# Matmuls on 64 rows of the PE array: from alternating between its two halves into two PSUM banks, to one half after the other into one bank

## Chip, cores, metric

One core of a Trainium2 chip runs the whole program once. The metric is the device time of that run in microseconds (us), median of three runs.

## What is computed

Two transformer-like blocks of two layers each, on 512 tokens of width 1024, in float32. Only the mixer of the first block matters here. It has three branches: sliding-window attention, HGRN2 and a gated delta rule (GDN). The parts around the change are these:

```python
# HGRN2: per head, dk = 64
attn = einsum('bhtd,bhsd,bhtsd->bhts', q, k, decay)   # decay = exp(cum_t - cum_s), causal
# gated delta rule: per head, dk = 64
A  = where(strict, einsum('bnhtd,bnhsd->bnhts', k * beta, k) * L, 0)
qk = where(incl,   einsum('bnhtd,bnhsd->bnhts', q, k) * L, 0)
```

Each branch has four heads of dimension 64, and the kernel works on chunks of 128 tokens (the reference uses 64). So every product in question is 128x128 with a contraction over 64.

## The kernel before

The five engines run programs written by hand, joined by semaphores. `at[key]` is a mark (semaphore, count), `wait_ge` waits for it, and `own()` lets an engine wait for the completion of its own last instruction. Each phase has a `main` stream (gemms with weights from a ring of three DMA buffers) and side streams (`conv`, `gdn`, `att`, `hgrn`, `inv`, `mem`). `weave` interleaves their generator steps into one order, the same on all engines, from hand-given costs. The change leaves each step's counts of instructions and its declared costs as they are, and so this order too.

Head h sits in partitions 64*(h%2) to 64*(h%2)+63. Its matmul therefore uses only the upper or only the lower 64 rows of the PE array. One float32 matmul is two MATMUL records in the trace, each with its own weight load. PSUM has 8 banks of 128x512 float32. `take` hands out a stream's banks in turn and lets PE wait until the one it hands out has been read: `hgrn` has two (6 and 7), `gdn` two (2 and 3).

Three groups of matmuls are touched, in both layers of the first block:

- `diag` (`hgrn_pe`): k times q for 4 chunks x 4 heads, 16 matmuls a layer; DVE multiplies them by the identity into `ACC` (4 instructions of 512 columns).
- `lev` (`hgrn_pe`): 14 steps a layer (7 levels x 2 pairs of heads) of 8 matmuls; DVE copies their masked parts over `ACC` with two `copy_predicated` (line 168).
- `kk` (`gdn_pe`): 4 steps a layer of 8 matmuls; DVE turns them into `AT` (k k) and `G5` (q k), 8 instructions of 512 columns.

In all three, PE takes both banks of the pool first. It then alternates: a matmul on the upper rows into the first bank, one on the lower rows into the second. DVE reads each bank with a pattern that puts the heads in place. For the other matmuls of this shape, in `ob`, `vn` and `og`, the kernel already has the order that the change brings: heads `HO = (0, 2, 1, 3)` with `own()` before head 1. All matmuls and transposes of the side streams go through `mm` and `tr` (lines 103 and 109); gemms are line 570.

Of the kernel before, what the change touches and what calls it, by code (L numbers as in the profile page):

```python
# [8 lines left out]
I32 = mybir.dt.int32  # L9
ALU = mybir.AluOpType  # L10
# [27 lines left out]
HO = (0, 2, 1, 3)  # L38
# [177 lines left out]
def bc(ap, axis, n):  # L216
    v = ap.unsqueeze(axis)
    shape = list(v.shape)
    shape[axis] = n
    return v.to_broadcast(shape)  # L220
# [65 lines left out]
def program(nc, T, out):  # L286
    ctx = ExitStack()
    with ctx:
# [48 lines left out]
        at = Marks()  # L337
        bank_of, plans = {}, {}
# [6 lines left out]
        ident = cst[:, K_ID:K_ID + 128]  # L345
# [6 lines left out]
        LV = [cst[:, K_LV + 128 * i:K_LV + 128 * (i + 1)] for i in range(7)]  # L352
# [468 lines left out]
        ACC = ar(O_HG + 7168, 4, 512)  # L821
# [354 lines left out]
        def hgrn_dve(v, l):  # L1176
# [34 lines left out]
                sl = slice(128 * i, 128 * i + 128)  # L1211
                at["cum", l] = v.scan(CUM[:, sl], ones, Zb[:, sl], par=True)
            yield
            A5 = ACC.rearrange("p c (i h t) -> p c i h t", i=2, h=2)
            id4 = ident.unsqueeze(1).unsqueeze(1).to_broadcast([128, 2, 2, 128])
            for c in range(0, 4, 2):
                for p in range(2):
                    v.wait_ge(at["diag", l, c, p])
                    at["free", ("diag", l, c, p)] = v.tt(
                        A5[:, c:c + 2, :, p], bank_of["diag", l, c, p].rearrange("p (c i t) -> p c i t", c=2, i=2), id4, ALU.mult,  # L1220
                        par=True)
            yield

            def halves(n):
# [7 lines left out]
            for s in range(-2, 15):  # L1232
                if 0 <= s < 14:
                    _, (_, (ef, es), (xf, xs), (_, qs), (kf, _)) = halves(s)
                    v.wait_ge(at["levexp", l, s], at["lev", l, s - 2] if s > 1 else None)
                    v.tt(xs, qs, es, ALU.mult, par=True)
                    at["levx", l, s] = v.tt(xf, kf, ef, ALU.mult, par=True)
                if s + 2 < 14:
                    hb, ((cf, cs), (ef, es), _, _, _) = halves(s + 2)
                    ref = cf[:, :, hb - 1:hb].to_broadcast([128, 256 // hb, hb])  # L1240
                    if s >= 0:
                        v.wait_ge(at["levx", l, s])
                    v.tt(es, cs, ref, ALU.subtract, par=s > -2)
                    at["leve", l, s + 2] = v.tt(ef, ref, cf, ALU.subtract, par=True)
                if s == 13:
                    at["lev_dve", l] = v.now()
                if 1 <= s < 15:
                    lv, i = LEV[s - 1]
                    mk = bc(LV[lv].bitcast(I32), 1, 4)
                    for h in range(2):  # L1250
                        v.wait_ge(at["lev", l, s - 1, h])
                        at["lev_acc", l] = at["free", ("lev", l, s - 1, h)] = v.pred(
                            A5[:, :, i, h], mk, bank_of["lev", l, s - 1, h].rearrange("p (c t) -> p c t", c=4))
                yield
            v.wait_ge(at["ecum", l])
            v.tt(BQ, BQ, E_, ALU.mult, par=True)
# [27 lines left out]
        def hgrn_pe(pe, l):  # L1284
            yield (5 if l == 0 else 9, 5 if l == 0 else 7)
            yield (3.5, 0)
            for c in range(0, 4, 2):
                pair = [take(pe, ("diag", l, c, p), "hgrn") for p in range(2)]
                pe.wait_ge(at["cum", l], at["hz", l])
                for u in range(4):  # L1290
                    ti, cs = u % 2, slice((c + u // 2) * 128, (c + u // 2) * 128 + 128)
                    for p in range(2):
                        rows = slice(64 * p, 64 * p + 64)
                        at["diag", l, c, p] = pe.mm(pair[p][:, u * 128:(u + 1) * 128], [(KT3[rows, ti, cs], BQ3[rows, ti, cs])])
            yield (2.8, 0)
            for s in range(-2, 15):
                if 1 <= s < 15:
                    lv, i = LEV[s - 1]
                    X3 = XV[:, 512 * i:512 * i + 512]
                    pair = [take(pe, ("lev", l, s - 1, h), "hgrn") for h in range(2)]  # L1300
                    pe.wait_ge(at["levx", l, s - 1])
                    for c in range(4):
                        for h in range(2):
                            x = X3[64 * h:64 * h + 64, c * 128:(c + 1) * 128]
                            at["lev", l, s - 1] = at["lev", l, s - 1, h] = pe.mm(pair[h][:, c * 128:(c + 1) * 128], [(x, x)])
                yield (3.2, 0.7)
            yield (3.8, 3)
            yield (1.3, 1.1)
            for m in range(0, 4, 2):
                bank = take(pe, ("kd", l, m), "hgrn")  # L1310
                pe.wait_ge(at["kdec", l])
                for u in range(4):
                    at["kd_t", l, m] = pe.tr(bank[:, u * 128:(u + 1) * 128],
                                             KT3[:, u % 2, (m + u // 2) * 128:(m + u // 2) * 128 + 128], ident)
            yield (1.5, 0)
            for c in range(6):
                if c < 4:
                    b, b2 = take(pe, ("ob", l, c), "hgrn"), take(pe, ("os", l, c), "hgrn")
                    pe.wait_ge(at["kd", l], at["hv", l])
                    for h in range(4):  # L1320
                        pr, ti = (h % 2) * 64, h // 2
                        hs = slice(64 * h, 64 * h + 64)
                        at["os", l, c] = pe.mm(b2[pr:pr + 64, ti * 64:ti * 64 + 64], [(KD[:, c, hs], BV3[:, c, hs])])
                    pe.wait_ge(at["st", l, c], at["lev_acc", l])
                    for h in HO:
                        pr, ti = (h % 2) * 64, h // 2
                        hs = slice(64 * h, 64 * h + 64)
                        if h == 1:
                            pe.own()
                        at["ob", l, c] = pe.mm(b[:, hs], [  # L1330
                            (ACC[:, c, h * 128:(h + 1) * 128], BV3[:, c, hs]),
                            (BQ3[pr:pr + 64, ti, c * 128:(c + 1) * 128], STs[c % 2][pr:pr + 64, ti, :])])
                if c in (3, 5):
                    finish_pe(pe, l, "h", c - 3, OB)
                yield (2.2, 1.5)
# [65 lines left out]
        def gdn_pe(pe, l):  # L1401
# [31 lines left out]
                        at["tr_t", l, m, half] = pe.tr(bank[:, u * 128:(u + 1) * 128],  # L1433
                                                       src[:, (u % 2) * 128:(u % 2) * 128 + 128], ident)
            yield (0, 1.1)
            for n in range(4):
                m0, which = n // 2 * 2, n % 2
                pair = [take(pe, ("kk", l, n, p), "gdn") for p in range(2)]
                pe.wait_ge(at["tr", l, m0 + 1])
                for u in range(4):  # L1440
                    m, ti = m0 + u // 2, u % 2
                    for p in range(2):
                        rows = slice(64 * p, 64 * p + 64)
                        at["kk", l] = at["kk", l, n, p] = pe.mm(pair[p][:, u * 128:(u + 1) * 128], [
                            (TR[rows, m, 2 + ti, :], TR[rows, m, (4 if which == 0 else 0) + ti, :])])
                yield (2.4, 0)
            for m in range(4):
                yield (1.5, 0)
# [82 lines left out]
        def gdn_act(a, l):  # L1531
# [41 lines left out]
                yield  # L1573
            for m in range(5):
                if m:
                    a.wait_ge(at["tm_t", l, m - 1], at["kk", l])
                    at["tm", l, m - 1] = at["free", ("tm", l, m - 1)] = a.cp(TM[:, m - 1, :], bank_of["tm", l, m - 1][:, :], par=True)
                yield

# [47 lines left out]
        def gdn_dve(v, l):  # L1627
# [41 lines left out]
            for m in range(4):  # L1669
                v.wait_ge(at["tr_t", l, m, 0])  # L1670
                k = hd(TOK[:, m, 256:512])
                v.tt(k, k, bc(eD[:, 4 * m:4 * m + 4], 2, 64), ALU.mult, par=True)
                m0, which = m // 2 * 2, m % 2
                v.wait_ge(at["g5e", l, m0 + 1])
                if which:
                    v.own()
                for p in range(2):
                    a4, g4 = [z[:, m0:m0 + 2, :].rearrange("p m (i h t) -> p m i h t", i=2, h=2)[:, :, :, p] for z in (AT, G5)]
                    k4 = bank_of["kk", l, m, p].rearrange("p (m i t) -> p m i t", m=2, i=2)
                    v.wait_ge(at["kk", l, m, p])  # L1680
                    if which == 0:
                        t = v.stt(a4, k4, -1.0, g4, ALU.mult, ALU.mult, par=True)
                    else:
                        t = v.tt(g4, k4, g4, ALU.mult, par=True)
                    at["free", ("kk", l, m, p)] = t
                yield
            v.own()
            v.wait_ge(at["kk", l])
            for m in range(5):
                if m < 4:  # L1690
                    a4, t4 = [z[:, m, :].rearrange("p (h t) -> p h t", h=4) for z in (AT, TT)]
# [1314 lines left out]
```

## Time and profile before

| | |
|---|---|
| median of three runs | 4441.57 us (4433.45, 4441.57, 4442.74) |
| the profiled run's own time | 4433.45 us |
| its span in the profile | 4431.7 us |
| granted TensorE clock, mean over the span | 0.945 of 2.4 GHz |

The span is the time from the first to the last instruction in the profile; 1.75 us of the run lie outside it. Idle times in brackets in the views name what ended them.

### The profile page before, as it was taken

Reading aid. Unit: us, or ns where it says so; the run is one execution under the profiler, and the core shown is the slowest. Engines: PE = TensorE matmul, PEld = TensorE weight load, DVE = VectorE, ACT = ScalarE, POOL = GpSimd, SP = SyncE. Lnnn points to the kernel's source line nnn. Section 1 sums busy time; section 2 is a strip of 40 time slices with the busy share of each in tenths; the row PEclk is TensorE's granted clock in tenths of the full one; section 3 lists DMA queues with packets and bytes.
Section 4 is the critical chain, followed back from the end, with each engine's and each line's share of the span. In section 5 each row is a group of like instructions: output and inputs, shape, how many; then the busy total and the mean of one; then the engine's idle time right before and its main releaser. Section 6 shows DMA issues by size and latency. Waiting matters only on the chain.

```text
span 4431.7 us, 51774 instructions
## 1 busy us (share of the span) xinstructions
PE 4051.1 (91%) x20660; PEld 3326.6 (75%) x20660; DVE 2573.7 (58%) x4060; ACT 1639.0 (37%) x2880; POOL 107.7 (2%) x199
## 2 busy tenths in 40 slices
PE   5878979988879899999999999999899999999998
PEld 4757868867659778888888777767778787777776
DVE  6775455554675332346666744676566667445865
ACT  2343232233443232333434233453344343334532
POOL 0000000000000000000000000000000000000000
PEclk9978889999979799989999999999899999999999
DMA  6402135633202133323231233133242312231233
GB/s 219 148 15 67 44 119 189 191 124 96 72 10 77 58 95 96 98 93 105 81 105 58 81 91 91 53 108 119 70 132 78 109 60 84 81 91 62 78 105 121
DMA packets 216641, 417.93 MB, mean 94 GB/s; under 512 B 16384, under 2 KB 61472, under 8 KB 214608
## 3 DMA queue, kind: packets, MB, share of 16 engines
q1 hardware_dynamic: 197584, 335.12, 24.4%
q0 software_dynamic: 18816, 79.49, 5.2%
q8 instruction: 163, 2.67, 0.2%
q14 instruction: 78, 0.64, 0.0%
HBM read 378.89 MB, written 35.67 MB: 94 GB/s over the span
## 4 chain that ended last, share of the span: by engine, by line
PE 75%; DVE 15%; ACT 6%; DMA 2%; issue 2%; DVEq 0%; SPq 0%; ACTq 0%; POOLq 0%
PE ps L570 55%; PE ps L103 14%; DVE arena L120 4%; ACT arena L191 3%; PE ps L109 3%; DVE arena L135 3%; DVE spl L120 3%; PE ps L2142 2%; ACT sph L191 1%; DMA ring<-in_ada_w 1%; DVE sm L141 1%; DVE HF L120 1%; DVE X L120 1%; PE ps L2138 1%; DVE arena L129 0%
## 5 line engine op out<-in xcount | busy, mean ns | idle before, releaser
L120 DVE TENSOR_TENSOR spl<-ring,sph 128x1024 fp32r<-128x1024 f32 (+2 forms) x556 | 651.6, 1179 | 834.7 <-ACT sph L191 833.3
L191 ACT ACTIVATE sph<-ring 128x1024 fp32r<-128x1024 f32 (+2 forms) x556 | 562.2, 1021 | 878.6 <-PE ps L570 668.2
L570 PE MATMUL ps<-sph,HTh 128*128 128x512 f32 (+3 forms) x1728 | 685.5, 397 | 10.7 <-ACT sm L191 5.4
L570 PE MATMUL ps<-spl,HTh 128*128 128x512 f32 (+3 forms) x1728 | 638.6, 370 | 0.0
L570 PE MATMUL ps<-sph,HTl 128*128 128x512 f32 (+3 forms) x1728 | 637.5, 369 | 0.0
L191 ACT ACTIVATE arena<-ps 128x512 f32<-128x512 f32 (+2 forms) x574 | 316.9, 564 | 778.6 <-PE ps L570 479.2
L570 PE MATMUL ps<-HTh,sph 128*128 128x512 f32 x1376 | 548.4, 399 | 23.1 <-DVE spl L120 16.0
L570 PE MATMUL ps<-HTh,spl 128*128 128x512 f32 x1376 | 540.1, 393 | 0.0
L570 PE MATMUL ps<-HTl,sph 128*128 128x512 f32 x1376 | 540.0, 392 | 0.0
L103 PE MATMUL ps<-arena 64*128 64x128 f32 (+7 forms) x2328 | 410.5, 368 | 55.7 <-ACT arena L191 22.3
L570 PE MATMUL ps<-sph 128*128 128x512 f32 x992 | 402.4, 406 | 8.8 <-DVE spl L120 8.7
L570 PEld LDWEIGHTS ps<-sph,HTh 128*128 128x128 f32 x1728 | 339.2, 196 | 83.7 <-issue 32.9
L570 PE MATMUL ps<-sph,spl 128*128 128x512 f32 x992 | 391.8, 395 | 0.0
L103 PEld LDWEIGHTS ps<-arena 64*128 64x128 f32 (+2 forms) x2328 | 296.2, 211 | 127.2 <-issue 28.9
L570 PE MATMUL ps<-spl,sph 128*128 128x512 f32 x992 | 390.5, 394 | 0.0
L570 PEld LDWEIGHTS ps<-sph,HTl 128*128 128x128 f32 x1728 | 339.5, 196 | 62.9 <-issue 18.8
L570 PEld LDWEIGHTS ps<-spl,HTh 128*128 128x128 f32 x1728 | 338.4, 196 | 53.3
L570 PEld LDWEIGHTS ps<-HTh,sph 128*128 128x128 f32 x1376 | 261.4, 190 | 78.6 <-DVE spl L120 22.7
L570 PEld LDWEIGHTS ps<-HTh,spl 128*128 128x128 f32 x1376 | 260.9, 190 | 55.7
L570 PEld LDWEIGHTS ps<-HTl,sph 128*128 128x128 f32 x1376 | 261.3, 190 | 53.1 <-issue 1.0
L109 PE MATMUL ps<-cst,arena 128*128 128x128 f32 x1160 | 186.7, 298 | 117.9 <-ACT arena L191 73.2
L109 PEld LDWEIGHTS ps<-cst,arena 128*128 128x128 f32 x1160 | 146.4, 153 | 168.0 <-ACT arena L191 71.0
(195 smaller groups left out, 5293.6 us busy)
## 6 DMA issues: line engine op xcount, KB each, us to landing
ring<-in_w_in SPq DMA_DIRECT2D x264, 512.0 KB, 3.7
ring<-in_ada_w SPq DMA_DIRECT2D x96, 512.0 KB, 4.4
ring<-in_w_down SPq DMA_DIRECT2D x44, 512.0 KB, 3.3
ring<-in_w_gate SPq DMA_DIRECT2D x40, 512.0 KB, 4.2
ring<-in_w_up SPq DMA_DIRECT2D x40, 512.0 KB, 4.6
ring<-in_w_mem SPq DMA_DIRECT2D x32, 512.0 KB, 3.4
ring<-in_w_out SPq DMA_DIRECT2D x32, 512.0 KB, 3.7
ring<-in_w_br_ssd SPq DMA_DIRECT2D x32, 512.0 KB, 3.8
```

Source lines behind the costliest of these rows:

```text
L103: ins = self.e.matmul(o, l, r, start=i == 0, stop=stop)
L109: self.e.transpose(o, i, ident).then_inc(*self.done.up())
L120: self.e.tensor_tensor(o, a, b, op).then_inc(*self.done.up())
L135: self.e.scalar_tensor_tensor(out=o, in0=a, scalar=s1, in1=b, op0=op0, op1=op1).then_inc(*self.done.up())
L141: self.e.tensor_reduce(o, a, AX, op).then_inc(*self.done.up())
L191: self.e.activation(o, a, f, **kw).then_inc(*self.done.up())
L570: ins = pe.e.matmul(o, l, r, start=k0 == 0 and i == 0 and not b.pairs, stop=k0 + b.ks == b.kt and i == 3 * b.ks - 1 and (c0 > 0 or not b.p ...
L2138: pe.e.matmul(bank.rearrange("p (h t) -> p h t", h=4), NFr[0][:, :], bc(NFr[1 + d][:, :], 1, 4), start=True, stop=False)
L2142: ins = pe.e.matmul(bank[:, h * 128:(h + 1) * 128], AA[:, m, h0 + h:h0 + h + 1].to_broadcast([128, 128]), tri, start=False, stop=h == 3)
```

## The change

It gives up the alternation. `diag` now fills one bank per chunk with the four heads in the order 0, 2 (upper rows), `own()`, 1, 3 (lower rows). `lev` fills one bank per two chunks: two matmuls on the upper rows, `own()`, two on the lower ones. `kk` fills one bank per chunk m and kind (k k or q k), in the order of `diag`, and its step m waits for the transposes of chunk m alone. Banks are taken one at a time. The numbers of matmuls (16, 112, 32 a layer) and of DVE instructions stay; their patterns change, and DVE waits for its own previous instruction before each `G5` product (four a layer, before two and one after them).

```diff
-            for c in range(0, 4, 2):
-                pair = [take(pe, ("diag", l, c, p), "hgrn") for p in range(2)]
+            for c in range(4):
+                bank = take(pe, ("diag", l, c), "hgrn")
                 pe.wait_ge(at["cum", l], at["hz", l])
-                for u in range(4):
-                    ti, cs = u % 2, slice((c + u // 2) * 128, (c + u // 2) * 128 + 128)
-                    for p in range(2):
-                        rows = slice(64 * p, 64 * p + 64)
-                        at["diag", l, c, p] = pe.mm(pair[p][:, u * 128:(u + 1) * 128], [(KT3[rows, ti, cs], BQ3[rows, ti, cs])])
+                for h in HO:
+                    pr, ti = (h % 2) * 64, h // 2
+                    if h == 1:
+                        pe.own()
+                    at["diag", l, c] = pe.mm(bank[:, h * 128:(h + 1) * 128], [
+                        (KT3[pr:pr + 64, ti, c * 128:(c + 1) * 128], BQ3[pr:pr + 64, ti, c * 128:(c + 1) * 128])])
...
-                    pair = [take(pe, ("lev", l, s - 1, h), "hgrn") for h in range(2)]
-                    pe.wait_ge(at["levx", l, s - 1])
-                    for c in range(4):
+                    for c in range(0, 4, 2):
+                        bank = take(pe, ("lev", l, s - 1, c), "hgrn")
+                        pe.wait_ge(at["levx", l, s - 1])
                         for h in range(2):
-                            x = X3[64 * h:64 * h + 64, c * 128:(c + 1) * 128]
-                            at["lev", l, s - 1] = at["lev", l, s - 1, h] = pe.mm(pair[h][:, c * 128:(c + 1) * 128], [(x, x)])
+                            for u in range(2):
+                                x = X3[64 * h:64 * h + 64, (c + u) * 128:(c + u + 1) * 128]
+                                if h and not u:
+                                    pe.own()
+                                at["lev", l, s - 1] = at["lev", l, s - 1, c] = pe.mm(
+                                    bank[:, (2 * u + h) * 128:(2 * u + h + 1) * 128], [(x, x)])
...
-            for n in range(4):
-                m0, which = n // 2 * 2, n % 2
-                pair = [take(pe, ("kk", l, n, p), "gdn") for p in range(2)]
-                pe.wait_ge(at["tr", l, m0 + 1])
-                for u in range(4):
-                    m, ti = m0 + u // 2, u % 2
-                    for p in range(2):
-                        rows = slice(64 * p, 64 * p + 64)
-                        at["kk", l] = at["kk", l, n, p] = pe.mm(pair[p][:, u * 128:(u + 1) * 128], [
-                            (TR[rows, m, 2 + ti, :], TR[rows, m, (4 if which == 0 else 0) + ti, :])])
+            for m in range(4):
+                for which in range(2):
+                    bank = take(pe, ("kk", l, m, which), "gdn")
+                    pe.wait_ge(at["tr", l, m])
+                    for h in HO:
+                        pr, ti = (h % 2) * 64, h // 2
+                        if h == 1:
+                            pe.own()
+                        at["kk", l, m, which] = pe.mm(bank[:, h * 128:(h + 1) * 128], [
+                            (TR[pr:pr + 64, m, 2 + ti, :], TR[pr:pr + 64, m, (4 if which == 0 else 0) + ti, :])])
                 yield (2.4, 0)
...
-                    for h in range(2):
-                        v.wait_ge(at["lev", l, s - 1, h])
-                        at["lev_acc", l] = at["free", ("lev", l, s - 1, h)] = v.pred(
-                            A5[:, :, i, h], mk, bank_of["lev", l, s - 1, h].rearrange("p (c t) -> p c t", c=4))
+                    for c in range(0, 4, 2):
+                        v.wait_ge(at["lev", l, s - 1, c])
+                        at["lev_acc", l] = at["free", ("lev", l, s - 1, c)] = v.pred(
+                            A4[:, c:c + 2], mk, bank_of["lev", l, s - 1, c].rearrange("p (c h t) -> p c h t", c=2, h=2))
```

## Rows read from the trace of the kernel before

**Rows 1.** The page: its head and its chain by engine.
```profile
span 4431.7 us, 51774 instructions
...
PE 75%; DVE 15%; ACT 6%; DMA 2%; issue 2%; DVEq 0%; SPq 0%; ACTq 0%; POOLq 0%
```
**Rows 2.** Windows: busy (records) of PE, PEld, DVE, ACT, POOL; clock; DMA share, GB/s.
```profile
264.00:280.00 16.00, 12.49 (x58) 9.22 (x58) 10.97 (x24) 6.30 (x17) 0.00 (x0) 0.53 0.01 2
...
364.00:400.00 36.00, 32.59 (x186) 28.16 (x186) 16.52 (x30) 14.01 (x25) 0.56 (x1) 0.71 0.18 59
```
**Rows 3.** Waits of PE from 240 to 365 us: total us, times, longest.
```profile
PE ps L109 <- ACT arena L191: 12.3, 4, 4.9
...
PE ps L103 <- DVE sm L120: 4.7, 1, 4.7
...
PE ps L103 <- DVE arena L168: 2.5, 1, 2.5
PE ps L103 <- DVE sm L135: 1.9, 1, 1.9
```
**Rows 4.** The chain that ended last, 262 to 284 us: start, us, what.
```profile
264.08 5.51 PE ps L103 x24
...
281.97 1.14 PE ps L103 x16
283.11 1.32 DVE arena L168 x2
```
**Rows 5.** The same chain, a piece near 296 us, then 339 to 365 us.
```profile
295.80 1.09 PE ps L103 x16
...
340.96 2.01 PE ps L103 x16
...
345.07 5.01 PE ps L103 x52
...
356.99 1.21 DVE HF L135 x2
...
358.33 5.68 PE ps L103 x20
```
**Rows 6.** Timeline, two `kk` steps on PE: start, us, engine, line, form, records.
```profile
348.91 1.16 PE L103 MATMUL ps<-X 64*128 64x128 f32 x16
...
358.33 2.08 PE L103 MATMUL ps<-X 64*128 64x128 f32 x16 [5.56 <-DVE HF L135]
```
**Rows 7.** Timeline, PE on products of all 128 rows, one after another.
```profile
269.51 1.97 PE L109 MATMUL ps<-cst,arena 128*128 128x128 f32 x8
...
277.95 1.12 PE L109 MATMUL ps<-cst,arena 128*128 128x128 f32 x4
...
409.53 0.39 PE L103 MATMUL ps<-X,arena 128*128 128x128 f32 x2
409.75 0.39 PE L103 MATMUL ps<-arena,X 128*128 128x128 f32 x2
```
**Rows 8.** Timeline, PE before and after `own()` in an `ob` step.
```profile
375.26 0.69 PE L103 MATMUL ps<-sm,arena 64*128 64x64 f32 x2
376.00 0.69 PE L103 MATMUL ps<-arena 128*128 128x64 f32 x2
```
**Rows 9.** Timeline, a `lev` step on PE and its two DVE reads.
```profile
312.96 3.35 PE L103 MATMUL ps<-arena 64*128 64x128 f32 x19
...
315.15 1.33 DVE L168 COPY_PREDICATED arena<-cst,ps 128x512 f32<-128x512 int32 x2
```
**Rows 10.** PE groups by form in 331.2 to 331.75 us: busy, mean ns.
```profile
L103 PE MATMUL ps<-arena 64*128 64x256 f32 x4 | 1.0, 376 | 0.0
L103 PE MATMUL ps<-arena 64*128 64x128 f32 x5 | 0.7, 286 | 0.0
```
**Rows 11.** The chain at `diag` of the second layer.
```profile
1153.76 1.28 DVE arena L120 x2
...
1155.17 2.02 PE ps L103 x24
```

More of the change, by code:

```diff
@@ L1213, in hgrn_dve @@
             yield
-            A5 = ACC.rearrange("p c (i h t) -> p c i h t", i=2, h=2)
-            id4 = ident.unsqueeze(1).unsqueeze(1).to_broadcast([128, 2, 2, 128])
-            for c in range(0, 4, 2):
-                for p in range(2):
[L1218 to L1221, printed above, removed]
+            for c in range(4):
+                v.wait_ge(at["diag", l, c])
+                at["free", ("diag", l, c)] = v.tt(
+                    ACC[:, c, :].rearrange("p (h t) -> p h t", h=4), bank_of["diag", l, c].rearrange("p (h t) -> p h t", h=4),
+                    bc(ident, 1, 4), ALU.mult, par=True)
             yield
@@ L1248, in hgrn_dve @@
                     lv, i = LEV[s - 1]
-                    mk = bc(LV[lv].bitcast(I32), 1, 4)
-                    for h in range(2):
-                        v.wait_ge(at["lev", l, s - 1, h])
-                        at["lev_acc", l] = at["free", ("lev", l, s - 1, h)] = v.pred(
-                            A5[:, :, i, h], mk, bank_of["lev", l, s - 1, h].rearrange("p (c t) -> p c t", c=4))
+                    A4 = ACC.rearrange("p c (i h t) -> p c i h t", i=2, h=2)[:, :, i]
+                    mk = LV[lv].bitcast(I32).unsqueeze(1).unsqueeze(1).to_broadcast([128, 2, 2, 128])
+                    for c in range(0, 4, 2):
+                        v.wait_ge(at["lev", l, s - 1, c])
+                        at["lev_acc", l] = at["free", ("lev", l, s - 1, c)] = v.pred(
+                            A4[:, c:c + 2], mk, bank_of["lev", l, s - 1, c].rearrange("p (c h t) -> p c h t", c=2, h=2))
                 yield
@@ L1286, in hgrn_pe @@
             yield (3.5, 0)
-            for c in range(0, 4, 2):
-                pair = [take(pe, ("diag", l, c, p), "hgrn") for p in range(2)]
+            for c in range(4):
+                bank = take(pe, ("diag", l, c), "hgrn")
                 pe.wait_ge(at["cum", l], at["hz", l])
-                for u in range(4):
-                    ti, cs = u % 2, slice((c + u // 2) * 128, (c + u // 2) * 128 + 128)
-                    for p in range(2):
-                        rows = slice(64 * p, 64 * p + 64)
-                        at["diag", l, c, p] = pe.mm(pair[p][:, u * 128:(u + 1) * 128], [(KT3[rows, ti, cs], BQ3[rows, ti, cs])])
+                for h in HO:
[4 more added lines that the diff above has]
+                        (KT3[pr:pr + 64, ti, c * 128:(c + 1) * 128], BQ3[pr:pr + 64, ti, c * 128:(c + 1) * 128])])
             yield (2.8, 0)
@@ L1435, in gdn_pe @@
             yield (0, 1.1)
-            for n in range(4):
-                m0, which = n // 2 * 2, n % 2
-                pair = [take(pe, ("kk", l, n, p), "gdn") for p in range(2)]
-                pe.wait_ge(at["tr", l, m0 + 1])
-                for u in range(4):
-                    m, ti = m0 + u // 2, u % 2
-                    for p in range(2):
-                        rows = slice(64 * p, 64 * p + 64)
-                        at["kk", l] = at["kk", l, n, p] = pe.mm(pair[p][:, u * 128:(u + 1) * 128], [
-                            (TR[rows, m, 2 + ti, :], TR[rows, m, (4 if which == 0 else 0) + ti, :])])
+            for m in range(4):
[8 more added lines that the diff above has]
+                            (TR[pr:pr + 64, m, 2 + ti, :], TR[pr:pr + 64, m, (4 if which == 0 else 0) + ti, :])])
                 yield (2.4, 0)
@@ L1575, in gdn_act @@
                 if m:
-                    a.wait_ge(at["tm_t", l, m - 1], at["kk", l])
+                    a.wait_ge(at["tm_t", l, m - 1], at["kk", l, 3, 1])
                     at["tm", l, m - 1] = at["free", ("tm", l, m - 1)] = a.cp(TM[:, m - 1, :], bank_of["tm", l, m - 1][:, :], par=True)
@@ L1672, in gdn_dve @@
                 v.tt(k, k, bc(eD[:, 4 * m:4 * m + 4], 2, 64), ALU.mult, par=True)
[L1673 to L1680, printed above, removed]
+                v.wait_ge(at["g5e", l, m])
+                for which in range(2):
+                    v.wait_ge(at["kk", l, m, which])
                     if which == 0:
-                        t = v.stt(a4, k4, -1.0, g4, ALU.mult, ALU.mult, par=True)
+                        t = v.stt(AT[:, m, :], bank_of["kk", l, m, 0][:, :], -1.0, G5[:, m, :], ALU.mult, ALU.mult, par=True)
                     else:
-                        t = v.tt(g4, k4, g4, ALU.mult, par=True)
-                    at["free", ("kk", l, m, p)] = t
+                        t = v.tt(G5[:, m, :], bank_of["kk", l, m, 1][:, :], G5[:, m, :], ALU.mult)
+                    at["free", ("kk", l, m, which)] = t
                 yield
-            v.own()
-            v.wait_ge(at["kk", l])
+            v.wait_ge(at["kk", l, 3, 1])
             for m in range(5):
```

## The prediction

> **What bounds the kernel now.** I read the page first. PE makes up 75% of the chain that ended last, DVE 15% [rows 1]. The average says little here, because all three groups sit in the mixers of the first block. So I went through the mixers by windows, waits and chain.
>
> From about 240 to 365 us (and again in the second layer, where every reading below repeats unless I say otherwise; I looked it up and don't show it) no engine is full. The chain jumps between PE, DVE and ACT, and PE runs much of the time at the lower of its two clock levels: 264 to 280 us shows a granted clock of 0.53, nearly all of it at 1.2 GHz [rows 2]. PE also waits a lot there, four times for ACT (12.3 us) and singly for DVE for 4.7, 2.5 and 1.9 us [rows 3]. The reader should see two kinds of touched steps. In some the chain runs through their matmuls; in others PE idles soon after, so that a longer step is hidden.
>
> **What one touched step costs now.** A `lev` or `kk` step is 8 matmuls, 16 records. It spans 1.16 us at the full clock and 2.08 us at the lower one [rows 6]. Products on all 128 rows, which nothing can run beside, start one per 0.22 us, two records of 0.11 [rows 7]. Eight would take 1.8 us, so the 1.16 us show that upper and lower rows now work side by side: eight turns of 0.11 plus about 0.27 to fill and drain. At the lower clock four more transposes take 1.97 - 1.12 = 0.85 us, a turn of 0.21 [rows 7].
>
> **What one costs after.** Two matmuls on the same rows are a block of four turns. At full clock that is 1.16 less four turns, 0.71; a block has half as many record starts to offset, so I take 0.68. At the lower clock it is 2.08 - 0.85 = 1.23. Behind `own()` the next matmul starts about 0.05 us after the last one ends: 375.26 + 0.69 = 375.95, next at 376.00 [rows 8]. A step is then: upper block of bank one, `own()`, lower block of bank one beside the upper block of bank two (other rows, other bank, no wait between them), `own()`, lower block of bank two. That is three blocks and two handovers. Full clock: 3 x 0.68 + 0.1 = 2.15, 1.0 us more than now. Lower clock: 3 x 1.23 + 0.1 = 3.8, 1.7 us more.
>
> That the middle blocks really overlap I take from 331.2 to 331.75 us, where four records of 64x256 on one half and five of 64x128 on the other ran in the same 0.55 us [rows 10].
>
> The Trainium skill (TensorE: Matmul & The Clock Gate, Part 3, The mechanism) says that matmuls start and end strictly in program order. By that rule a step would lose three more turns, which is the rival "in order" below. The finer records of that stretch speak against the rule: there the third product on one half starts before the second in the program, on the busy half.
>
> **The sum.** I take each touched step of a layer where it lies. `lev` steps are counted from 0.
>
> - PE stays the chain behind the step, so all of it counts. At the lower clock `lev` 2 at 264.08 [rows 4], `lev` 3 (same pattern, 12 us later) and `lev` 12 at 340.96 [rows 5]: 3 x 1.7 = 5.1. At full clock `lev` 6 at 295.80 and `lev` 13, which lies with `kk` 0 and `kk` 1 in the 5.01 us from 345.07 [rows 5]: 2 x 1.0.
> - `kk` 0 and 1: 2 x 1.0, less 0.25 because `kk` 0 may start when the first of two transposed banks is copied out. `kk` 3 waits for two DVE reads of 0.6 us each and then runs at the lower clock [rows 5, 6]. It will need only the first read to begin: 1.7 - 0.6 = 1.1. Together 2.85.
> - The chain leaves PE for the two reads of the step. Then the finer banks help: the first read (0.67 us [rows 9]) runs while the last block still computes. `lev` 4 [rows 4], full clock: second bank ready at 2.15, its read over at 2.85, against 1.19 + 1.34 = 2.53 now, so 0.35. `lev` 8 at 312.96, lower clock: 3.8 + 0.7 = 4.5 against 3.4 [rows 9], so 1.05. Together 1.4. Its 2.08 us end only 0.1 before the read at 315.15, so it has no slack.
> - `diag`: the second half waits for two DVE reads of 1.28 us together and has PE's chain behind it [rows 11]. It may start one read, 0.64, earlier; its own growth is 1.0 and a little is lost at the first half: about 0.5.
> - Hidden: `lev` 0, 1 and 5 are followed by PE idle times of 2.5, 4.7 and 1.9 us [rows 3], more than their 1.7, 1.7 and 1.0. `lev` 7, 9, 10, 11 come before the waits for ACT [rows 3], and their reads follow 1.6 to 4.3 us later. `kk` 2 ends 4 us before its reads on the chain at 356.99 [rows 5] and before the 5.56 us idle time [rows 6]. If all that cover were gone: 1.7 x 4 + 1.0 x 4 = 10.8 a layer, an upper bound.
> - The DVE patterns: still 512 columns per instruction, and the nearest row, two reads in 1.33 us [rows 9], already has four separate pieces per partition. I see no reason for a gain or a loss: 0. The additional waits of DVE for itself (one more a layer) are idle gaps of well under 0.1 us: 0. Semaphore waits on PE are inside the handover.
>
> Sum per layer: 5.1 + 2.0 + 2.85 + 1.4 + 0.5 = 11.9, two layers 24 us. Nothing catches it up later: the weight ring is full and the next phase needs the mixers' output, so the rest shifts. The profiled run took 4433.45 us, with its span of 4431.7 [rows 1]; it becomes 4457. The median of the three runs lies 8.1 above it, and I assume that this scatter stays: 4441.6 + 24 = 4465.6, rounded to 4465.
>
> **The rivals.**
>
> *In order.* The middle blocks do not overlap except for one turn, three turns more per step: 0.33 at full clock, 0.64 at the lower. Per layer 3 x 0.64 + 2 x 0.33 on PE, 2 x 0.33 + 0.64 for `kk`, 0.33 + 0.64 for the reads: 4.9. Total 24 + 10 = 34, 4475. For it: upper and lower blocks will now come in whole blocks of eight instructions, not alternating. Against: rows 10. The Trainium skill's rule, cited above, is this case.
>
> *Cover lost.* The hidden steps show, because PE's idle times there wait for ACT or DVE work that itself stems from a touched step. In the second layer the idle time behind `lev` 9 is under 1 us. Half of the 10.8 a layer gives 24 + 11 = 35; all of it with "in order" 24 + 22 + 10 = 56, 4497.
>
> *Absorbed.* DVE paces the mixers wherever it is nearly full, each bank is handed over earlier, and PE stays at the full clock in the touched steps. Every 1.7 becomes 1.0: 5.0 + (0.75 + 1.0 + 0.4) + 0.7 + 0.4 = 8.3 a layer, 17 us. If the chain turns to DVE behind half of it, 8 us or less: 4449, no change that can be told. For it: single reads are 0.67 us and start earlier. Against: three of the largest terms lie on PE stretches with nothing of DVE beside them.
>
> *The other side: the clock.* PE is busy for longer in these stretches, and the granted clock may stay at its upper level there and behind. From 364 to 400 us PE is busy 32.6 of 36 us at a mean clock of 0.71 [rows 2], so 0.58 of it runs at half speed, 21 us. At full speed that would save 10 a layer. In 264 to 280 us, 12.5 us busy at 0.53 [rows 2], it would save 5 or 6. Against the 17 us that the change costs when all is at full clock, this gives 17 - 32 = -15, 4427. It decides only if more than half of those low stretches are lifted in both layers. Against it: at 358.33 the clock is low just behind 5.56 us of idle time [rows 6], which the change doesn't fill, and the same low stretch stands in both layers.
>
> **How the numbers follow.** A kernel like this can be told from no change from about 0.2%, 8.9 us. Forecast (slower by some 24, between 15 and 30) 0.55; in order or cover lost (30 to 56) 0.25; absorbed 0.14; clock 0.06. Absorbed splits: 0.10 within 0.2%, 0.04 still slower than that. The clock splits: 0.03 faster, 0.03 within. So faster 0.03, same 0.13, slower 0.84. The range runs from 4447 (most of absorbed left out below) to 4490 (short of everything going wrong together). The predicted time is that of the likeliest, 4465.
>
> **What the profile after would show.** A `kk` or `lev` step spans about 2.15 us at full clock and 3.8 at the lower instead of 1.16 and 2.08 [rows 6]; 2.5 and 4.4 would mean "in order". The weight loads gain some 80 idle pieces of 0.2 us released by PE itself. The first read of a `lev` step begins before PE's last block ends. `kk` 3 starts 0.6 us earlier behind `kk` 2's first read. The stretch from `lev` 2 to the end of `kk` 3 grows by 10 to 12 us in each layer; from 365 us to the end of each mixer all durations are as before. The forecast is wrong if the steps grow and the stretch does not (absorbed), or if the mean clock there rises (the clock).

## The result, and the profile after

The changed kernel takes 4471.88 us (median of 4 runs, 4469.27 to 4477.11) against 4440.84 for the kernel before in the same comparison: ratio 1.0079, 95% interval 1.0065 to 1.0091, so 29 to 40 us slower, about 35 (the two medians lie 31 apart). A later comparison gave 1.0085 (1.0068 to 1.0101). The sign and the place were as forecast. The size is half as large again as the 24 us of the sum, inside the stated range.

The profiled run's span is 41.9 us longer than in [rows 1]. The page after, its head and its chain by engine:

```profile
span 4473.6 us, 51742 instructions
...
PE 76%; DVE 14%; ACT 6%; DMA 2%; issue 2%; DVEq 0%; SPq 0%; POOL 0%; ACTq 0%; POOLq 0%
```

A `kk` step of the kernel after at full clock, in the timeline, where [rows 6] had 1.16 us:

```profile
369.50 2.33 PE L103 MATMUL ps<-X 64*128 64x128 f32 x16
...
370.26 0.53 PEld L103 LDWEIGHTS ps<-X 64*128 64x128 f32 x8 [0.25 <-PE ps L103]
...
371.11 0.52 PEld L103 LDWEIGHTS ps<-X 64*128 64x128 f32 x4 [0.32 <-PE ps L103]
```

The weight loads stop twice for PE itself, and between the stops lie 4, 8 and 4 records. The chain shows the same three blocks in `lev` 12, at the lower clock, where [rows 5] had one piece of 2.01, and in `kk` 3:

```profile
353.93 1.16 PE ps L103 x4
...
355.14 1.32 PE ps L103 x8
...
356.51 1.22 PE ps L103 x4
...
378.74 0.61 DVE HF L135
...
379.40 1.23 PE ps L103 x4
...
380.68 1.32 PE ps L103 x8
```

The middle block has twice the records of the others and takes 1.32 us, not twice 1.2: lower and upper rows do run side by side. `kk` 3 starts behind one read of 0.61 us instead of two [rows 5]. From 240 to 1400 us the loads' waits for PE's own matmuls grew from 16 pieces, 3.7 us, to the first row below: 76 more, where some 80 had been forecast, of 0.36 us each instead of 0.2. The second row is DVE's idle time before the `lev` reads, before 10.3 us in 4 pieces:

```profile
PEld ps L103 <- PE ps L103: 30.8, 92, 0.5
```
```profile
PE ps L103: 24.9, 18
```

Where the time went, by windows. The first fence is the kernel before: the two mixers, cut at the same ACT instructions in both kernels, then two short stretches of the first mixer, around `lev` 6 and around `kk` 0 with `lev` 13. The second is the kernel after. Columns as in [rows 2]: length, busy (records) of PE, PEld, DVE, ACT, POOL, granted clock, DMA share, GB/s.

```profile
165.40:371.80 206.40, 152.71 (x959) 121.09 (x958) 145.37 (x286) 78.45 (x197) 0.56 (x1) 0.80 0.19 58
1149.90:1330.90 181.00, 142.29 (x941) 111.38 (x941) 130.33 (x261) 79.62 (x200) 0.53 (x1) 0.85 0.13 40
...
285.00:298.30 13.30, 9.93 (x69) 6.55 (x66) 10.61 (x27) 9.16 (x25) 0.00 (x0) 0.87 0.00 1
...
344.10:349.00 4.90, 4.07 (x40) 2.45 (x38) 3.31 (x7) 0.82 (x2) 0.00 (x0) 1.00 0.00 0
```
```profile
167.80:392.80 225.00, 180.90 (x953) 136.57 (x954) 145.46 (x283) 79.18 (x197) 0.56 (x1) 0.75 0.17 51
1172.80:1372.80 200.00, 171.00 (x941) 128.60 (x940) 131.57 (x261) 80.21 (x199) 0.53 (x1) 0.80 0.12 36
...
292.10:309.60 17.50, 14.60 (x70) 10.24 (x69) 11.49 (x28) 9.19 (x24) 0.00 (x0) 0.66 0.00 0
...
358.80:369.60 10.80, 10.10 (x39) 5.51 (x37) 3.15 (x6) 0.87 (x2) 0.00 (x0) 0.51 0.00 0
1336.80:1347.70 10.90, 10.19 (x40) 5.53 (x38) 3.43 (x6) 0.87 (x2) 0.00 (x0) 0.50 0.01 2
```

The mixers grew by 18.6 and 19.0 us, 37.6 of the 41.9; the rest lies in stretches whose code is the same. And the granted clock fell, though PE is busy longer. With two levels, 1.0 and 0.5, a mean of 0.80 over 206.4 us is 83 us at the lower level, and 0.75 over 225 us is 113: 30 us more in the first mixer, by the same reckoning 26 in the second. The stretch of `lev` 6 grew by 4.2 us, forecast 1.0; that of `kk` 0 and `lev` 13 by 5.9, forecast 1.75; there the clock went from 1.00 to 0.51.

The first mixer in six stretches, again cut at the same ACT instructions, with the touched steps that the sum counts in each:

| before, us | steps counted | forecast | before: us, clock | after: us, clock | growth |
|---|---|---|---|---|---|
| 184.0 to 272.2 | `lev` 2 | 1.7 | 88.2, 0.81 | 89.2, 0.78 | 1.0 |
| 272.2 to 284.9 | `lev` 3, 4 | 2.05 | 12.7, 0.73 | 16.8, 0.64 | 4.1 |
| 284.9 to 303.9 | `lev` 6 | 1.0 | 19.0, 0.91 | 24.1, 0.72 | 5.1 |
| 303.9 to 344.0 | `lev` 8, 12 | 2.75 | 40.1, 0.79 | 42.7, 0.76 | 2.6 |
| 344.0 to 350.7 | `kk` 0, 1, `lev` 13 | 2.75 | 6.7, 1.00 | 13.6, 0.61 | 6.9 |
| 350.7 to 371.8 | `kk` 3 | 1.1 | 21.1, 0.66 | 20.4, 0.75 | -0.7 |

Three stretches grew by 10.3 us more than forecast, and in each of them the clock fell by 0.09 or more. The last one became shorter, and there the clock rose.

### The profile page after: what moved, and what is told of

It is laid out like the page before. It is cut to its first block, busy times and chain, and to the rows that moved or that the text cites. A ratio compares the mean times of both kernels' runs of the same rounds, so it can differ in the third digit from the quotient of the medians.

```text
span 4473.6 us, 51742 instructions
## 1 busy us (share of the span) xinstructions
PE 4114.7 (92%) x20660; PEld 3366.1 (75%) x20660; DVE 2576.1 (58%) x4060; ACT 1639.3 (37%) x2880; POOL 107.3 (2%) x199
## 3 DMA queue, kind: packets, MB, share of 16 engines
q1 hardware_dynamic: 197584, 335.12, 24.1%
## 4 chain that ended last, share of the span: by engine, by line
PE 76%; DVE 14%; ACT 6%; DMA 2%; issue 2%; DVEq 0%; SPq 0%; POOL 0%; ACTq 0%; POOLq 0%
PE ps L570 55%; PE ps L103 14%; DVE arena L120 3%; ACT arena L191 3%; PE ps L109 3%; DVE arena L135 3%; DVE spl L120 2%; PE ps L2139 2%; DMA ring<-in_ada_w 1%; ACT sph L191 1%; DVE sm L141 1%; DVE HF L120 1%; DVE X L120 1%; PE ps L2135 1%; ACT L191 0%
## 5 line engine op out<-in xcount | busy, mean ns | idle before, releaser
L103 PE MATMUL ps<-arena 64*128 64x128 f32 (+7 forms) x2328 | 450.1, 375 | 50.4 <-ACT arena L191 22.5
L103 PEld LDWEIGHTS ps<-arena 64*128 64x128 f32 (+2 forms) x2328 | 315.5, 211 | 138.2 <-issue 29.2
```

The lines of the kernel that those rows point to most:

```text
L103: ins = self.e.matmul(o, l, r, start=i == 0, stop=stop)
```

## The experiments

All ratios are to the kernel before on the same chip. The first three keep its banks and DVE instructions and change only PE's order and waits, in all three groups of matmuls.

**Blocks of two, no wait.** The order of the change, without `own()`, in the two old banks (each half has its own, so nothing has to wait).

```diff
-                for u in range(4):
+                for p, u in [(p, 2 * w + u) for w in range(2) for p in range(2) for u in range(2)]:
...
-                    for p in range(2):
```

> Kernel before with its banks and waits, but within each step PE takes two products on the upper rows, two on the lower, two upper, two lower; no own(). Theory 'side by side' (each half of the array runs ahead of the other): the four blocks still overlap, a step stays at about 1.2 us (2.1 at the lower clock), time within 0.2% of before, ratio 1.000. Rival 'in order': a block can overlap the next only by its last turn, 13 turns instead of 8 per step, +0.56 us (+1.07 at the lower clock); on the terms of the prediction about 14 us, ratio 1.003.

Measured 1.0007 (0.9998 to 1.0015): no change that can be told, at most 7 us. The timeline's `kk` 1:

```profile
354.76 1.26 PE L103 MATMUL ps<-X 64*128 64x128 f32 x16
```

1.26 us against 1.16, one turn of 0.11 more, where "in order" wanted five. So the order alone costs next to nothing.

**Blocks of four, no wait.** The same with `for p in range(2) for u in range(4)`.

> As the one before, with four products on the upper rows and then four on the lower. 'Side by side': the lower four still run beside the upper four, ratio 1.000, if the depth to which PE runs ahead reaches over 4 products (16 instructions with their weight loads). 'In order': 15 turns, +0.8 us (+1.5), about 20 us, ratio 1.0045. A depth smaller than that gives something between.

Measured 1.0055 (1.0043 to 1.0067), +24 us. The timeline at `lev` 6:

```profile
299.51 1.71 PE L103 MATMUL ps<-arena 64*128 64x128 f32 x16
```

1.71 us is five turns more than 1.16, so three of the first half's eight turns ran beside the second half's. The single records show when the free half starts. Here its first record starts at 0.55 us of the step, together with the fifth of the other half; with blocks of two it starts 0.01 us after the other half's first. In both, three records that stand ahead of it in the program have not started yet. PE runs ahead on the free half, but here only by about three records; both theories as worded fail. And with no wait added, these 13 turns cost 24 us, where 15 had been priced at 20; the mixers spend 179 us at the lower level in this run against 138 before.

**The change's order and waits in the old banks.** As the first, with `if p and u % 2 == 0: pe.own()`.

> Banks, DVE patterns and marks of the kernel before, with the order and the own() of the changed one: two upper, own(), two lower, two upper, own(), two lower. If the cost of the change is the step's length on PE, the steps are as in the changed kernel (2.33 us full clock, 3.86 low) and the time is not less than its 4472. If the earlier release of single banks helps as forecast (0.65 us at four places of a layer), it is about 5 us slower than the changed kernel, 4477, ratio 1.009. If instead bank layout or DVE patterns of the change cost time, it is faster than the changed kernel.

Measured 1.0092 (1.0079 to 1.0105), +41. The steps have the length of the changed kernel. The nominal excess over the change (1.0079) is what the earlier release of single banks was thought to be worth, but the intervals overlap, so this is not settled. The loss is there without the new bank layout and the new DVE patterns, so they are not its cause. Against blocks of two without the waits, the same kernel but for the waits, it is some 37 us slower.

**Waits alone.** The alternation stays; PE waits for itself before the second and fourth pair.

```diff
                     for c in range(4):
+                        if c % 2:
+                            pe.own()
                         for h in range(2):
```

> Kernel before with its alternation of the halves, and PE waiting for itself twice in each step (before the second and the fourth pair of products). It has the two handovers of the changed kernel and all of the side-by-side work of the old one. If a handover costs what the traces say (0.33 us from the last record's start to the next one's at full clock, 0.47 at the lower, against a turn of 0.11 or 0.21, and a slow first record), a step takes about 1.75 us (2.9 low) against 1.16 (2.08) before and 2.33 (3.86) changed: half of the growth. Time by proportion +16 to +20 us, ratio 1.004. Rival: the loss is that of the overlap alone and handovers are hidden; ratio 1.000 to 1.001.

Measured 1.0066 (1.0050 to 1.0082), +29: most of the loss, without giving up one side-by-side product. The timeline, `kk` 1, in which the clock rises (0.57 up to 360.3 us, 1.00 behind):

```profile
359.41 2.19 PE L103 MATMUL ps<-X 64*128 64x128 f32 x16
```

At the lower clock a step takes 3.0 us; one that lies at full clock as a whole takes 1.86 (`kk` 2, at 363.14) to 1.89 (`lev`). That is near the 1.75 and 2.9 expected, but the time grew by 29 us and not by 16 to 20. The clock has a share in it: by the profile's clock records the mixers spend 195 us at the lower level, as in the changed kernel, against 138 before. The rival (handovers hidden) is refuted.

**One part at a time.** `lev` alone, `kk` alone, `diag` alone, each as in the diff of the change.

> Only the lev part of the change. Read from the shifts between the two traces, lev has some 13 us of the 20 us by which each mixer grew in the profile, kk 5 and diag 1; scaled to the measured 33 us of the change: lev alone +22 to +26 us, ratio 1.0055. Rival: by the forecast's own terms (lev 8.4 of 11.9 a layer at the old clock levels) +17, ratio 1.004. If the parts are not additive because the clock falls only with all of them, less than that.

> Only the kk part of the change. Theory: lev alone gave +25 us, the whole +35; kk has most of the rest, +7 to +9 us, ratio 1.0018. By the forecast's terms 2.85 a layer, +6, ratio 1.0013. If the parts share one loss (a clock that is already low), kk alone may give more than the difference, up to +12.

> Only the diag part. Forecast term 0.5 a layer: +1, ratio 1.000. lev alone gave 1.0057 and kk alone 1.0007 of the 1.0079, so if parts add up it is 1.0015 (+6); if they don't, the rest is the clock that falls with all of them together.

Measured: `lev` 1.0057 (1.0044 to 1.0069), `kk` 1.0007 (0.9997 to 1.0016), `diag` 1.0005 (0.9996 to 1.0014). Within their intervals they add up to the whole, 1.0069. `lev` alone costs 25 us (20 to 31), more than the 17 of the forecast's own terms. `kk` alone costs +3 us, less than both its figures, but its interval reaches 7 and so doesn't exclude the 6 of the forecast.

The profile of `lev` alone holds a comparison that nobody planned: the same stretch around `lev` 6, the same instructions, in both layers.

```profile
292.80:310.40 17.60, 14.63 (x71) 10.36 (x70) 11.47 (x29) 9.26 (x25) 0.00 (x0) 0.66 0.00 0
1268.90:1283.50 14.60, 13.51 (x70) 9.29 (x70) 11.48 (x28) 9.44 (x25) 0.00 (x0) 0.77 0.01 1
```

3.0 us apart, and the clock with them: 12 us at the lower level in one, 7 in the other. The experiment with the old banks and the change's waits has the same for `kk` 0:

```profile
359.10:366.00 6.90, 5.69 (x39) 3.22 (x37) 4.01 (x7) 0.87 (x2) 0.00 (x0) 1.00 0.00 0
1335.90:1347.20 11.30, 10.30 (x40) 5.67 (x38) 3.50 (x7) 0.92 (x3) 0.00 (x0) 0.50 0.00 1
```

**Filling PE's idle time.** Extra products of constants into a bank that is overwritten next anyway.

```diff
+        def fill(pe, bank, n):
+            for _ in range(n):
+                pe.e.matmul(bank[:, :], cst[:, 0:128], cst[:, 0:512], start=True, stop=True)
...
                         bank = take(pe, ("pt", l, n - 2, kt), "att")
+                        fill(pe, bank, 1 if kt == 0 else 0)
```

> Kernel before, with extra 128x512 products of constants into the bank that the next step overwrites, issued where PE idles anyway in the mixers: 2, 1 and 2 ahead of lev 0, 1, 2, one ahead of each transpose of attention probabilities, three ahead of kk 3. Theory 'clock counts': the time at the lower clock inside the mixers (83 and 55 us of 206 and 181) falls by a third or more, and the kernel gets faster by 5 to 15 us, ratio 0.997 to 0.999. Rival: the clock does not follow these fills, and they only delay: ratio 1.000 to 1.003.

> The changed kernel with the same fills (2, 1, 2 ahead of lev 0 to 2, one ahead of each transpose of probabilities, two ahead of kk 3). The changed kernel spends 30 and 27 us more at the lower clock in its mixers than the one before. If that is part of its loss, of its 35 us 10 or more go: ratio to the kernel before 1.005. If the lower clock only accompanies the loss, ratio stays 1.008 or rises.

Measured 1.0016 (1.0007 to 1.0026) and 1.0097 (1.0082 to 1.0112). The low-clock time in the mixers did fall, in the kernel before from 138 to 107 us and in the changed one from 195 to 150, and the time still rose: the fills ahead of `kk` 3 alone lengthened their stretch by 3.3 us a layer. These two were too blunt. So the fills were cut to the 16 ahead of the transposes of probabilities:

> The changed kernel with one extra 128x512 product of constants ahead of each transpose of attention probabilities only (16 in all), where PE waits 1.9 to 4.1 us for ACT. In the profiles so far the stretch around lev 6 takes 17.6 us with 11.9 us at the lower clock and 14.4 us with 3.4; the one of kk 0 takes 10.8 with 10.6 and 6.9 with none. If the fills lift the clock in one of the two places per layer, 3 to 4 us a layer go: 3 to 8 us faster than the changed kernel, ratio to before 1.006 to 1.007. If the clock does not follow, 1.008 or more.

> The kernel before with the same 16 extra products. Together with the more numerous fills it was 1.0016; most of that came with the three ahead of kk 3 (its stretch grew by 3.3 us a layer) and those ahead of lev. With these 16 alone: the low-clock time in 298 to 344 us of the old trace falls (it fell from 17 to 7 us with all fills) and the time is 1 to 5 us less, ratio 0.999 to 1.000: the one variant here that might beat the kernel before. Rival: each fill costs its own 0.4 to 0.9 us somewhere, +4, ratio 1.001.

The changed kernel came to 1.0067 (1.0053 to 1.0081), median 4464.17 instead of 4471.88. The intervals overlap, so the times alone prove nothing. The windows: both mixers, then the stretches of `lev` 6 and `kk` 0 in the first layer:

```profile
167.00:384.90 217.90, 179.58 (x967) 132.42 (x966) 144.87 (x283) 78.80 (x198) 0.56 (x1) 0.80 0.17 53
1161.50:1365.10 203.60, 176.75 (x957) 129.56 (x956) 131.61 (x261) 80.26 (x199) 0.53 (x1) 0.81 0.11 36
...
292.10:307.40 15.30, 14.30 (x72) 8.98 (x71) 11.47 (x28) 9.11 (x25) 0.00 (x0) 0.78 0.00 1
354.60:361.20 6.60, 5.69 (x39) 3.21 (x38) 4.00 (x7) 0.89 (x3) 0.00 (x0) 1.00 0.00 0
```

With the clock back at 0.80, the first mixer grew by 11.5 us over the 206.4 before instead of 18.6. `kk` 0 takes 6.6 us instead of 10.8. The second mixer goes the other way: it grew by 22.6 us instead of 19.0, though its `lev` 6 kept the clock (14.4 us at 0.88 instead of 16.7 at 0.74); `kk` 0 stayed at the lower level (10.9 us at 0.50). So the windows show what the clock is worth in single stretches; the fills as a whole don't prove its share of the loss. The kernel before with these fills: 0.9995 (0.9987 to 1.0004), the same; its low-clock time from 298 to 344 us did not fall as expected. No variant here beats the kernel before.

**The changed kernel once more.**

> The changed kernel once more, unaltered. Its first profile was 42 us longer than that of the kernel before, while the times differ by 35. If the excess over the forecast's 24 us is the clock in the stretches of lev 6 and kk 0, the step lengths are again 2.33 and 3.86 us, and the growth of each mixer goes with the low-clock time found in these stretches: about 12 us where both stay at full clock, 18 to 19 where both fall. Ratio again 1.0065 to 1.009. If the excess has another cause, the growth is 18 to 19 us a mixer whatever the clock does.

```profile
167.00:389.60 222.60, 179.16 (x951) 134.86 (x950) 145.87 (x284) 79.22 (x198) 0.56 (x1) 0.76 0.17 52
...
291.80:306.60 14.80, 13.70 (x72) 9.39 (x71) 11.51 (x29) 9.51 (x25) 0.00 (x0) 0.77 0.00 1
355.50:366.40 10.90, 10.19 (x39) 5.55 (x38) 3.14 (x5) 0.91 (x3) 0.00 (x0) 0.51 0.00 0
```

Ratio 1.0085. This time `lev` 6 of the first layer kept more of the clock (14.8 us at 0.77 instead of 17.5 at 0.66) and `kk` 0 did not. The mixer grew by 16.2 us, near the forecast's 11.9 and the 4 us of `kk` 0. The second mixer, where both fell, grew by 21.0, 2 us more than the expectation's upper figure. Over the two profiles of the changed kernel growth goes with the clock of these stretches roughly, not to the microsecond; with the fills the second mixer doesn't fit: with `kk` 0 alone of the two at the lower level the same account gives 11.9 + 4, about 16, and 22.6 were measured.

## Why the forecast was right, and what was too small

- *PE now works on both halves at once; a step goes from 8 turns to three blocks and two handovers.* Right. Forecast 2.15 and 3.8 us, measured 2.33 and 3.86. The 0.18 is mostly the middle block: in the chain of `kk` 1 the pieces are 0.72, 0.81 and 0.71 us with 0.04 and 0.05 between them, against three of 0.68 and 0.05. Blocks were priced a little short, handovers not.
- *The middle blocks overlap.* Right (8 records in 1.32 us). "In order" is refuted: a step in blocks of two takes 1.26 us, where it wanted 1.7. The rule of the Trainium skill (TensorE: Matmul & The Clock Gate, Part 3, The mechanism) that matmuls keep strict program order in start and end does not hold here between halves. What the runs put in its place is a short lead, about three records.
- *Which steps lie on the chain and which are hidden.* Right in the main. The stretch of `lev` 0 and 1 (240 to 262 us in the first layer) did not grow at all in either layer. Cover was used up elsewhere as expected: the idle time before `kk` 3 went from 5.56 to 4.29 us, the wait behind `lev` 5 from 1.92 to 0.62. The rival "cover lost" isn't needed for the first mixer; in the second, where 2 us stay unexplained in the later profile, it stays open.
- *The sum, 11.9 a layer.* With the fills, the first mixer had the mean clock of before, 0.80, and grew by 11.5 us. That looks like the sum come out, but it is in part luck: `lev` 3 and 4 grew by 4.3 us there (priced 2.05), and `lev` 12, priced 1.7 at the lower level, ran at full clock and its stretch became 0.4 shorter.
- *The finer release of banks gives some time back.* The profile shows it (`kk` 3 starts behind one read). Its worth, 5 us in total, agrees with 1.0092 against 1.0079 but isn't shown.
- *Each step at the clock level that it had before.* This is the term that was mis-sized. `lev` 6 was priced at 1.0 and the pair `kk` 0, `lev` 13 at 1.75, both at full clock. Where the clock held as before, they cost 1.1 and 1.7 to 2.0 us (with `lev` 6 at 0.77 or 0.78 instead of 0.87, 1.3 to 2.0). In the first profile after, both ran at the lower level for most of the time or all of it and cost 4.2 and 5.9. That is 3.2 + 4 us in the first layer and 2.4 + 4 in the second (16.7 and 10.9 us there), 13.6 together. With the slightly longer steps, estimated at 2 us, the sum is 24 + 13.6 + 2 = 39.6 against 37.6 measured in the mixers. It is not complete: `lev` 3 and 4 cost 2 us a layer more than priced, and the last stretch of the table, with `kk` 3, became shorter instead of growing.
- *The signs in the profile.* The idle pieces of the weight loads and the step lengths came as written. The stretch from `lev` 2 to the end of `kk` 3 grew by 21 and 19 us in the two layers, not by 10 to 12. From 365 us to the end of the mixer the durations were not as before: both layers won 1.7 to 1.8 us there, with 4.4 us less at the lower level.
- *The rival "the clock" had the wrong sign.* It argued that a PE busy for longer may keep its clock. The busy time in the first mixer rose from 152.7 to 180.9 us of a longer stretch, and the clock fell. The added busy time of this change is the same products spread over more time, in part with one half of the rows at work and with the pauses of the handovers between. That this is why the clock fell is not shown.
- *`lev` and `kk`.* `lev` alone cost 25 us (20 to 31) against 17 on paper: its terms were too small. `kk`, 2.85 a layer on paper, cost 3 us for both layers when alone, and the clock of its stretch stayed at 1.00 in that profile; up to 7 us are within the interval. With `lev` alone changed, that stretch ran at the lower level in both layers, as in the changed kernel.

Shown: the waits that PE makes for itself cost the time. With the order and the banks held equal they take the ratio from 1.0007 to 1.0092, with all pairing kept they cost 1.0066, and the order of the products alone costs next to nothing. The clock's share is read from pairs of identical stretches and from the fills in one layer, not from an experiment that holds the clock everywhere; why it falls in one of two identical stretches stays open. With blocks of two and no wait, too, 4.7 us of the `kk` 0 stretch of the first layer lay at the lower level, and it was 2 us longer than before, though no `own()` had been added.

## What to carry to other kernels

Products that use half the rows of the array paired up by themselves here, each half writing to its own bank; blocks of two are as good as strict alternation, blocks of four are not. What costs is PE waiting for its own last matmul, even with all the pairing kept: in `kk` 1 of the changed kernel 0.33 and 0.40 us pass from the start of the last record before the wait to the start of the next, against 0.11 inside a block. And when a change spreads PE's work over more time in a stretch where its clock moves between two levels, price each step at both levels; here the sum fell short by about a third of the loss, most of it in stretches whose clock fell.

## What was not expected of the hardware

- PE runs ahead on a free half of the rows by about three records: a step takes 1.26 us in blocks of two, 1.71 in blocks of four, 1.16 in strict alternation.
- The granted clock fell with a higher busy share: 0.80 at 152.7 of 206.4 us busy, 0.75 at 180.9 of 225.0. Identical instructions 976 us apart ran at 0.66 and 0.77.
- Two pauses per step, with all pairing kept, cost 29 us, where the whole change costs 35; and the low-clock time rose with them from 138 to 195 us.
- Blocks of four, with no pause at all, cost 24 us.
